# Routing map of a product-key expert layer: one comparison for four tokens, and the weight moved to the other factor

## The reference, cut to what matters

```python
sv, si = lax.top_k(s, PEER_TOPK)                      # the 16 best of 128 keys, per head and half
cand = sv[:, :, 0, :, None] + sv[:, :, 1, None, :]
cv, ci = lax.top_k(cand.reshape(...), PEER_TOPK)      # the 16 best pairs
i1 = jnp.take_along_axis(si[:, :, 0], ci // PEER_TOPK, axis=-1)
i2 = jnp.take_along_axis(si[:, :, 1], ci % PEER_TOPK, axis=-1)
e = i1 * N_KEYS + i2
g = jax.nn.softmax(cv, axis=-1)
```

## Time and profile before

| | |
|---|---|
| median of 3 runs | 4747.7 us (4745.55 to 4752.98) |
| the profiled execution | 4749.57 us |
| its span, first to last instruction | 4748.0 us |
| PE, PEld busy | 3653.2 and 2972.0 us (77% and 63%) |
| DVE, ACT, POOL busy | 2798.0, 1306.3 and 1459.3 us (59%, 28%, 31%) |
| granted TensorE clock, mean | 0.869 of full |

### The profile page before, as it was taken

How to read it: one execution, slowest core, us unless ns; L and a number is a source line. 1 busy time by engine, 2 the same in 40 slices (tenths; PEclk the granted TensorE clock), 3 DMA queues, 4 the chain that set the end, 5 groups by cost and what they waited for, 6 DMA issues and landing times. The chain is left out here.

```text
span 4748.0 us, 62801 instructions
## 1 busy us (share of the span) xinstructions
PE 3653.2 (77%) x20229; PEld 2972.0 (63%) x20229; DVE 2798.0 (59%) x6033; ACT 1306.3 (28%) x3080; POOL 1459.3 (31%) x1307
## 2 busy tenths in 40 slices
PE   6899777765566869455540799999999999999995
PEld 1344255551125558445540799999999988889994
DVE  0111166440013230488889788888888888888885
ACT  0111033330001010067650332333333333333331
POOL 0000000000000032077750454455554544555440
PEclk9999878887876979766665999999999999999997
DMA  8443254109971122134450888888888888888884
GB/s 320 152 169 132 82 164 142 62 27 412 416 288 50 59 66 72 50 82 103 100 124 2 303 297 291 302 308 316 302 302 298 297 307 307 306 302 300 300 295 156
DMA packets 404735, 992.91 MB, mean 209 GB/s; under 512 B 185860, under 2 KB 254303, under 8 KB 341896
## 3 DMA queue, kind: packets, MB, share of 16 engines
q1 hardware_dynamic: 338168, 479.00, 29.2%
q0 software_dynamic: 64144, 474.73, 27.3%
q10 hardware_dynamic: 2272, 37.68, 2.1%
HBM read 906.36 MB, written 152.04 MB: 223 GB/s over the span
## 5 line engine op out<-in xcount | busy, mean ns | idle before, releaser
L1201 PE MATMUL e_pa<-k_hi_d,e_uh 128*128 128x320 f32 x2048 | 637.3, 311 | 179.7 <-POOL e_ul L2022 179.7
L1201 PE MATMUL e_po<-e_ph,e_vh 128*128 128x320 f32 x2048 | 662.7, 324 | 138.3 <-POOL e_vl L2026 102.7
L1202 PE MATMUL e_po<-e_pl,e_vh 128*128 128x320 f32 x2048 | 653.7, 319 | 0.0
L1203 PE MATMUL e_po<-e_ph,e_vl 128*128 128x320 f32 x2048 | 653.0, 319 | 0.0
L1202 PE MATMUL e_pa<-k_lo_d,e_uh 128*128 128x320 f32 x2048 | 633.7, 309 | 0.0
L1203 PE MATMUL e_pa<-k_hi_d,e_ul 128*128 128x320 f32 x2048 | 633.7, 309 | 0.0
L2031 POOL DMA_INDIRECT e_uv<-peer_uv,k_g_idx x416 | 398.7, 958 | 622.5 <-DVE e_pY L1974 583.6
L1962 DVE CUSTOM_DVE_ANT_0 e_uv<-e_uv,e_pH 128x1024 f32<-128x1024 f32 x416 | 504.0, 1211 | 100.3 <-DMA e_uv<-peer_uv,k_g_idx 99.5
L1974 DVE SCALAR_TENSOR_TENSOR e_pY<-e_uv,e_wts,e_pY 128x1024 f32<-128x1024 f32 x412 | 526.5, 1278 | 0.0
L1994 DVE TENSOR_TENSOR e_act<-e_act,k_OT 128x320 f32<-128x320 f32 x256 | 390.2, 1524 | 215.5 <-ACT e_act L1895 215.5
L1201 PEld LDWEIGHTS e_pa<-k_hi_d,e_uh 128*128 128x128 f32 x2048 | 385.3, 188 | 188.3 <-issue 188.2
(11 more groups left out here) (283 smaller groups left out, 5465.9 us busy)
## 6 DMA issues: line engine op xcount, KB each, us to landing
s_kv<-kv_pages SPq DMA_DIRECT2D x128, 512.0 KB
s_kv<-kv_state SPq DMA_DIRECT2D x32, 2048.0 KB, 17.1
e_u<-peer_ut SPq DMA_DIRECT2D x128, 512.0 KB
e_v<-peer_uv SPq DMA_DIRECT2D x128, 512.0 KB, 6.0
s_g<-r_G SPq DMA_DIRECT2D x10, 4096.0 KB
k_OT<-s_g SPq DMA_DIRECT2D x128, 320.0 KB, 3.3
k_win_sample<-state_k_win ACTq DMA_DIRECT2D x28, 1168.0 KB
v_win_sample<-state_v_win POOLq DMA_DIRECT2D x28, 1168.0 KB, 9.5
```

Of the source, the lines that this page charges most:

```text
L1201: nc.tensor.matmul(out, lhs_hi, rhs_hi, start=start, stop=False)
L1202: nc.tensor.matmul(out, lhs_hi, rhs_lo, start=False, stop=False)
L1203: return nc.tensor.matmul(out, lhs_lo, rhs_hi, start=False, stop=stop)
```

## The change

DVE makes `hot1` for all four tokens of a group in one comparison of 4 x 128 elements, without the weight; one operand is the iota, which is copied once into the unused quarter of the PSUM tile `r_pp`. The weight goes into `hot2`: POOL multiplies by it in a second operation of the same instruction (and copies two lists instead of one into `second`), and ACT makes only `hot2` for token 3, now with the weight.

```diff
-        off = sb("r_off", [P, 2, SLOTS, NK])
-        second = sb("r_second", [P, SLOTS, GT])
+        off = sb("r_off", [P, SLOTS, NK])
+        second = sb("r_second", [P, 2, SLOTS, GT])
...
                     v.wait_ge(spread, NGT * i + g + 1)
-                    for t in range(GT - 1):
-                        col = slice(GT * g + t, GT * g + t + 1)
-                        x = nc.vector.tensor_scalar(hot1[:, g % SLOTS, t], keep.iota[:], pickT[:, 0, col], pickT[:, 2, col],
-                                                    ALU.is_equal, ALU.mult)
-                    x.then_inc(hot1_done, 1)
+                    nc.vector.tensor_tensor(hot1[:, g % SLOTS], pp[:, 3 * P:4 * P].unsqueeze(1).to_broadcast([P, GT, NK]),
+                                            pickT[:, 0, GT * g:GT * g + GT].unsqueeze(2).to_broadcast([P, GT, NK]),
+                                            ALU.is_equal).then_inc(hot1_done, 1)
...
+                step(v, dve, nc.vector.tensor_copy(pp[:, 3 * P:4 * P], keep.iota[:]))
                 search(0, P, lambda: None)
...
-                        for n in range(2):
-                            x = nc.scalar.activation(off[:, n, u], keep.iota[:], ACT.Abs, scale=-1.0,
-                                                     bias=pickT[:, n, col])
-                        x.then_inc(off_done, 1)
+                        nc.scalar.activation(off[:, u], keep.iota[:], ACT.Abs, scale=-1.0, bias=pickT[:, 1, col]
+                                             ).then_inc(off_done, 1)
...
-                        nc.scalar.activation(hot1[:, u, GT - 1], off[:, 0, u], ACT.Relu, scale=pickT[:, 3, col],
-                                             bias=pickT[:, 2, col])
-                        nc.scalar.activation(hot2[:, u, GT - 1], off[:, 1, u], ACT.Relu, scale=-1.0,
-                                             bias=keep.ones[:, 0:1]).then_inc(last_done, 1)
+                        nc.scalar.activation(hot2[:, u, GT - 1], off[:, u], ACT.Relu, scale=pickT[:, 3, col],
+                                             bias=pickT[:, 2, col]).then_inc(last_done, 1)
...
-                        nc.gpsimd.tensor_copy(second[:].rearrange("p s t -> p (s t)"),
-                                              pickT[:, 1, ds(GT * g, GT * SLOTS)]).then_inc(second_done, 1)
+                        nc.gpsimd.tensor_copy(second[:].rearrange("p n s t -> p n (s t)"),
+                                              pickT[:, 1:3, ds(GT * g, GT * SLOTS)]).then_inc(second_done, 1)
...
                             for t in range(GT - 1):
-                                x = nc.gpsimd.tensor_scalar(hot2[:, u, t], keep.iota[:], second[:, u, t:t + 1], None,
-                                                            ALU.is_equal)
+                                x = nc.gpsimd.tensor_scalar(hot2[:, u, t], keep.iota[:], second[:, 0, u, t:t + 1],
+                                                            second[:, 1, u, t:t + 1], ALU.is_equal, ALU.mult)
```

## The result

The changed kernel took 4789.8 us (median of 4 runs, 4785.6 to 4795.4) against 4750.3 of the kernel before, measured beside it: a ratio of 1.0085, interval [1.0067, 1.0102], 32 to 48 us slower. I had forecast 28 us faster. The sum as a function of d, the price of GpSimd's second operation with its pointer, comes within 5 us of the measured loss once d is read off: it is 0.19 us, not 0.

The account below looks back on a forecast made before the run. VectorE was taken to set each routing tile. Two outer tiles at 3.9 plus three middle ones at 7.0 give 28.8, less 0.8 for copies: 28 off 4747.7, forecast 4720 us, range 4710 to 4795.

Parts of the forecast that it names:

- The sum as a function of d: Routing stage's change in us: -40 + 435 times the price of GpSimd's second operation, from 0.05 on; nil at 0.092.
- The middle row: Possible price of GpSimd's second operation, between 0 and 0.29 us: 0.107, what a second pointer costs ScalarE.
- The rival on the other side: GpSimd becomes the bound because the multiply costs per element: at 0.29 us +86, 4834; decides from 0.114; chance 0.34.
- the margin of 1.9 us: First tile: GpSimd's last factor ends at 2096.72, VectorE's last row at 2098.62, so GpSimd is 1.9 us from being last.
- the other case: GpSimd's second operation costs 0: 28 us gained, 4720, own range 4712 to 4732; chance 0.46 for prices below 0.07.
- VectorE's part: One comparison per group at 0.61 us replaces three taking 0.83: saves 7.0 us per tile, 35 if VectorE stays last.
- its chains of 76.5 and 85.8: VectorE's time per tile after saving 7.0 us: 76.5 in the first and last tile, 85.8 in the three between.
- ScalarE's part: Per group one of two distances and one factor of two go; lighter, but worth nothing by itself.
- GpSimd's relief: GpSimd's delay from VectorE's present rows in a tile: 2.0 us taken as gone, at most 2.7, of 11.5 over undisturbed.
- the long operations: VectorE's 2048-element operations with two SBUF inputs, where GpSimd loses 8.8 us in the first tile; taken to stay.
- the stage: Routing map, built from 2022 to 2462 us of a 4748 us span; its gain moves the end by the same amount.
- Issue: VectorE's waits at the top of its loop's three further turns, 10.1 us a turn, 30.3 together; expected to stay.

Follow-up runs that it names:

- experiment 1: The changed kernel with GpSimd's comparison alone, one operation and one pointer, weight left out for three tokens of four: 4723.8 us, ratio 0.9932.
- experiment 2: The changed kernel with GpSimd's second operation multiplying by the constant 1.0 instead of a weight through a second pointer: 4757.0 us, ratio 1.0007.
- experiment 4: The changed kernel with two of a group's four hot2 factors made by ScalarE and two by GpSimd, full computation: 4717.3 us, ratio 0.9926.
- experiment 7: The kernel before with only GpSimd's part of the change, the wider copy and the multiplication: 4811.3 us, ratio 1.0129.
- experiment 3: The changed kernel with the iota of VectorE's comparison read from SBUF instead of PSUM: 4841.7 us, ratio 1.0185.
- experiment 8: The changed kernel with GpSimd's comparison alone (weight left out for three tokens of four) and VectorE's iota in SBUF: 4764.8 us, ratio 1.0026.
- experiment 5: The changed kernel with the search's two 2048-element comparisons of a tile also reading their iota from PSUM: 4779.4 us, ratio 1.0060.
- experiment 6: The kernel of experiment 4 with the search's two comparisons also reading their iota from PSUM: 4712.8 us, ratio 0.9920.

## Why the prediction was wrong

The step that failed is the price of GpSimd's second operation, the value of d: "I take 0 as the single likeliest value, because of those 0.30 us, in which a second stage has room". It measured 0.193. That one operation costs 0.30 more than a copy was no sign of room: the second operation came on top with 0.11, and its pointer with 0.08 (experiments 1 and 2). The middle row, ScalarE's second pointer at 0.107, was near the pointer alone, and I had priced pointer and operation as alternatives, where they add up. The Trainium skill, GPSIMD Engine Reference, "Performance pitfalls for Q7 kernels", has about 102 cycles for a read command that doesn't overlap the one before it, an estimated 0.085; the measured 0.08 of the pointer agrees with it in size. No run shows that a read command is what it pays for.

The rival on the other side is what happened: GpSimd becomes the bound, d above 0.114. I gave it 0.34, with the margin of 1.9 us as the reason for it, but the forecast stood on the other case. That the time lies inside 4710 to 4795 is due to that case's share in the range.

*VectorE's part.* Right: 0.59 for a row against my 0.61, and its chains of 76.5 and 85.8 came out at 75.5 and 85.7 where nothing else is last (experiment 4).

*ScalarE's part.* ScalarE got 16 us a tile lighter and the tiles got longer; nothing speaks against "worth nothing by itself", though no run has this part alone. I missed what it was good for: its free time is where the work belonged, and experiment 4 spends it.

*GpSimd's relief.* I took 2.0 us a tile and said at most 2.7. GpSimd's first tile took 73.7 in the kernel before and 70.6 in experiment 1, so 3.1 went there: what I had set down to the long operations and kept, 8.8, came down to 7.7. Between experiment 7 and the changed kernel it is 2.2 to 2.7. The rule of the Trainium skill, SBUF — State Buffer, "Who interferes with whom", is borne out: a row with two inputs in SBUF delays GpSimd (experiments 3 and 8), one with a PSUM input leaves most dozens at 9.30, and half of the delay at the long operations goes when two of four get a PSUM input (experiment 5).

*The sum.* With d = 0.193, -40 + 435d gives +44; measured are +39.4 by the medians and +46.7 in the stage of the profiled executions. Tile by tile: 98.1 forecast for the first and 96.4 measured, 97.6 and 98.6 to 99.6 for the three between. I had also said that the end moves by as much as the stage does. The traces bear that out only roughly: from the end of the stage to the end of the span are 2284.5 us in the kernel before, 2278.1 in the changed one, 2286.6 in experiment 1 and 2273.4 in experiment 3, less where the stage is longer. No run shows why. "Issue" stayed as said. With d = 0, experiment 1 gave the forecast itself.

So the reasoning about chains held, and one price that no row of the trace showed decided the sign. A margin of 1.9 us before 96 instructions a tile bears 0.02 us on each, and by my own formula the whole gain is gone at 0.092, less than the middle row's 0.107; I should have weighed the unknown price by that.

## What to carry to other kernels

Before work goes to another engine, take that engine's margin to the end of the stage and divide it by the number of instructions that get dearer: if an unknown price of a few hundredths of a microsecond uses it up, work out at what price the whole gain is gone and time that one instruction first. A second operation in a GpSimd instruction isn't free because it is a field of the same instruction; count the operation and its pointer as two terms. Where GpSimd runs beside VectorE and ends the stage, a broadcast constant that VectorE reads is worth a place in PSUM (experiments 3 and 5); where VectorE ends it, the same edit gave nothing that could be told (experiment 6).

## What the runs showed of the hardware

- GpSimd's scalar operation on 128x128 fp32, from start to start: 0.582 us with one comparison and one pointer (experiment 1), 0.693 with a multiplication by a constant as well (experiment 2), 0.775 with a multiplication by a second pointer (the changed kernel).
- A VectorE comparison of 128x512 has a median of 0.69 us whether its iota lies in PSUM or in SBUF (the longest 0.69 and 0.96), but GpSimd beside it needs 9.30 to 9.92 or 9.97 to 11.77 us for the same twelve instructions (first six dozens of the changed kernel and of experiment 3).
- One VectorE operation of 128x2048 with both inputs in SBUF (2.28 us) stretches the GpSimd instruction beside it from 0.79 to 2.94 us, though they share no tile (the changed kernel).
